# Decoder layer with paged cache: value fetches of a sequence held, on both issuing queues, until the last four key blocks of the next sequence have landed

## The chip, the cores and the metric

One Trainium2 chip; the kernel runs on one of its cores. The metric is the device time of one launch in microseconds (us), lower is better. Where several runs are given, it is their median.

## The reference, cut to what matters

One layer of a hybrid decoder is computed for a prompt of 512 positions and for 8 decoding sequences with one new token each, which have 4096 past positions in a paged cache (128 positions to a page, 256 to a block, so 16 blocks a sequence). The change touches the decoding attention alone:

```python
def moba_sample(q, k, v, cache_k, cache_v, page_table):
    ...
        k_full = cache_k[page_table[:, :own_first]].astype(f32).reshape(Bd, n_full, MOBA_BLOCK, H, D)
        kmean = jnp.mean(k_full, axis=2)
        gate = jnp.einsum('bhtd,bnhd->bhtn', qf, kmean)
        _, sel = lax.top_k(gate, topk)
        ...
        kg = cache_k[pages, :, hidx].reshape(Bd, H, T, topk * MOBA_BLOCK, D)
        vg = cache_v[pages, :, hidx].reshape(Bd, H, T, topk * MOBA_BLOCK, D)
        ...
    p = jax.nn.softmax(jnp.concatenate(scores, axis=-1), axis=-1)
    ...
```

All keys of a sequence are read, since every block's mean key is compared with the query. Of the values only those of the three best blocks of each of the 8 heads are read. Everything else of the layer is there too: one input projection of 1024 by 3584 (seven pieces of 512 columns: k, q, v, u, va, ga, gb), the prompt's own attention, the chunked gate of group A, the output projection, norms, and the rows k, v and sgu_v as outputs.

## The kernel before, in words

**Engines and steps.** `make_plan` lists the steps of every engine in lanes (a lane is a list of steps in a fixed order), gives each step a duration and what it waits for, and merges the lanes of an engine greedily by a model clock. Each engine then issues its list in exactly that order. The model has a pseudo-engine Q for the DMA engines, with lanes for keys, values and weights. The plan only orders; what is waited for at run time are semaphores.

**Prompt.** For each of the seven projection pieces, TensorE does four tiles (`pj`, line 957, 8 matmuls each), and for the output projection eight tiles more (`op`, line 1047, 64 matmuls). ScalarE (`ACT`) evacuates, GpSimd (`POOL`) makes the reciprocal roots (`rstd`, lines 833 and 834), VectorE (`DVE`) scales. Prompt attention (`qk`, `ptr`, `pv`, lines 1003, 1012 and 1024) lies between the projection pieces.

**Decoding, for each sequence b of 8.**
1. `ld`: GpSimd issues 16 indirect DMAs of 512 KB (line 820), one for each key block, into K, which is there once. They may start when step `ex` of the sequence before has read K to the end (`s_ext`). Each block has a semaphore `s_k[n]`.
2. `ks`: VectorE adds the two halves of each block (line 684); `gs`: TensorE sums them over partitions, four blocks at a time (line 1063).
3. `ga`, `pg`: VectorE multiplies by the query, picks the top three and their pages (lines 1445 to 1480); the page numbers stand in selT and raise `s_sel`.
4. `ex`, `sr`: VectorE multiplies the picked key blocks by the query (24 products, line 1492) and reduces (line 1507). When `ex` is done, the next sequence's keys may be loaded and SP spreads the next query row over the partitions (`qb`, line 748).
5. `bc`, `mt`, `mb`: bias, maximum, exponent, going through one PSUM bank DC (lines 1070 to 1079 on TensorE, 1512 to 1532 on VectorE, 1253 on ScalarE).
6. `fetch`: 48 DMAs of 32 KB bring the picked values into V, which is there once too. It is fetched by halves of heads (hh) and rank (k). For sequences 0 to 6, ranks 0 and 1 are issued by SP (32 DMAs) and rank 2 by GpSimd (16 DMAs); for the last sequence SP, GpSimd and ScalarE share them (`v_queue`). A half may be fetched when `pv0` or `pv1` of the sequence before has read it (`wait_v_free`). `fetch_v` reads page numbers from selT into registers (line 665) and issues (line 669).
7. `pv0`, `pv1`: TensorE multiplies the exponents by the values (line 1092), ScalarE copies out (lines 1276 and 1277), and SP gathers the rows (`obs`).

**What orders the value fetches.** Each engine's program is in order: SP's fetches stand between its other DMAs, GpSimd's behind the 16 key loads of the next sequence (the plan's `more` holds them back until `ld` 15 of b + 1 has been issued), and only `s_sel` and `wait_v_free` are waited for at run time.

After `pv1` of the last sequence a tail (`fin0` to `ffd`) finishes the sample rows: normalise, gate, output projection in two halves, norm, residual, store.

Of the kernel before, what the change touches and what calls it, by code (L numbers as in the profile page):

```python
# [17 lines left out]
B = 8  # L18
# [30 lines left out]
def make_plan():  # L49
# [175 lines left out]
    for b in range(B):  # L225
        for n in range(NB):
            deps = [("DVE", ("ex", b - 1, PARTS - 1))] if b else []
            add("POOL", "load", ("ld", b, n), 1.25, *deps)
            add("Q", "key", ("k", b, n), KEY_US, ("POOL", ("ld", b, n)))
            deps = [("Q", ("k", b, n))]  # L230
            if n < SUMS and b:
                deps.append(("DVE", ("sr", b - 1)))
            if n >= SUMS:
                deps.append(("PE", ("gs", b, (n - SUMS) // 4)))
            add("DVE", "gate", ("ks", b, n), 0.75, *deps)
        if b == 0:
            add("POOL", "load", ("const",), 8.5)
        for g in range(G):
            late = [("DVE", ("ks", b, n)) for n in range(4 * g, 4 * g + 4)]
            add("PE", "gate", ("gs", b, g), 1.0, *late, *([("DVE", ("ga", b - 1))] if b else []))  # L240
        used = [("Q", ("v", b - 2, hh, k)) for hh in range(2) for k in range(TOP)] if b >= 2 else []
        add("DVE", "gate", ("ga", b), 3.3, ("PE", ("gs", b, G - 1)), ("SP", ("qb", b)), *used)
        parts = [("ex", b, i) for i in range(PARTS)]
        for s in ([("pg", b)] + parts if b == B - 1 else parts[:1] + [("pg", b)] + parts[1:]) + [("sr", b)]:
            deps = [("ACT", ("mb", b - 1))] if s[0] == "sr" and b else []
            add("DVE", "gate", s, {"ex": 1.7, "pg": 1.2, "sr": 3.4}[s[0]], *deps)
        if b:
            add("SP", "spread", ("qb", b), 3.0, ("DVE", ("ex", b - 1, PARTS - 1)))
        add("PE", "score", ("bc", b), 0.3, ("DVE", ("pg", b)), ("DVE", ("sr", b)))
        add("DVE", "score", ("bc", b), 1.2, ("PE", ("bc", b)), ("POOL", ("const",)))  # L250
        add("PE", "score", ("mt", b), 0.3, ("DVE", ("bc", b)))
        add("DVE", "score", ("mt", b), 0.9, ("PE", ("mt", b)))
        add("PE", "score", ("mb", b), 0.3, ("DVE", ("mt", b)))
        add("DVE", "score", ("mb", b), 0.4, ("PE", ("mb", b)))
        add("ACT", "score", ("mb", b), 0.5, ("DVE", ("mb", b)))
        add("DVE", "score", ("pv0", b), 0.2, ("ACT", ("mb", b)))
        landed = []
        for hh in range(2):
            free = [("PE", (f"pv{hh}", b - 1))] if b else []
            landed.append([])  # L260
            for k in range(TOP):
                eng = v_queue(b, k)
                more = [("POOL", ("ld", b + 1, NB - 1))] if eng == "POOL" and b < B - 1 else []
                add(eng, "fetch", ("fetch", b, hh, k), 7.0, ("DVE", ("pg", b)), *free, *more)
                add("Q", "value", ("v", b, hh, k), 1.8, (eng, ("fetch", b, hh, k)))
                landed[hh].append(("Q", ("v", b, hh, k)))
        for hh in range(2):
            s = (f"pv{hh}", b)
            add("PE", "score", s, 1.4, ("ACT", ("mb", b)), ("DVE", ("pv0", b)), *landed[hh])
            stored = [("SP", ("obs", b - 2))] if b >= 2 and hh == 0 else []  # L270
            add("ACT", "score", s, 0.5 + 0.3 * hh, ("PE", s), *stored)
        add("SP", "gather", ("obs", b), 2.0, ("ACT", ("pv1", b)))
# [93 lines left out]
def hymba_kernel(nc, x_prompt, x_sample, cache_k, cache_v, page_table, g_pre, w_in, sgu_gain, sgu_w,  # L366
# [34 lines left out]
    with ctx:  # L401
# [284 lines left out]
        def wait_v(eng, b, hh):  # L686
# [3 lines left out]
            if by_pool:  # L690
                eng.wait_ge(s_vp[hh], 16 * 4 * 2 * by_pool)

        def wait_v_free(eng, b, hh):
            if b >= 1:
                eng.wait_ge(dc_full, dc_use[(f"pv{hh}", b - 1)] + 1)
# [3 lines left out]
        def _(sp):  # L699
# [18 lines left out]
            for s in PLAN["SP"]:  # L718
# [9 lines left out]
                elif kind == "vrow":  # L728
                    t = s[1]
                    if t < NT:  # L730
                        pa_evac_wait(sp, ("pj", 2, t))
                        sp.dma_start(vp_rows[t], v[:, t, :]).then_inc(s_vrow_stored, 16)
                    else:
                        sb_evac_wait(sp, ("sfd", 2))
                        sp.dma_start(vs_rows, vs[:, :]).then_inc(s_vrow_stored, 16)
                elif kind == "vns":
                    sp.wait_ge(s_vns, 1)
                    sp.dma_start(sv_rows, vns[:, :]).then_inc(s_vns_stored, 16)
                elif kind == "qst":
                    sb_evac_wait(sp, ("sfd", 1))  # L740
                    sp.dma_start(q_rows, qs[:, :]).then_inc(s_qst, 16)
                elif kind == "qb":
                    b = s[1]
                    if b == 0:
                        sp.wait_ge(s_qst, 16)
                    else:
                        sp.wait_ge(s_ext, b)
                    sp.dma_start(qb[:, :], q_rows[b:b + 1, :].broadcast_to([P, W])).then_inc(s_qb, 16)
                elif kind == "fetch":
                    b, hh, k = s[1:]  # L750
                    sp.wait_ge(s_sel, b + 1)
                    wait_v_free(sp, b, hh)
                    fetch_v(sp, b, hh, [k], "vs")
                elif kind == "obs":
                    b = s[1]
                    sp.wait_ge(dc_free, dc_use[("pv1", b)] + 1)
                    for j in range(4):
                        sp.dma_start(obs[b:b + 1, :].rearrange("b (t j d) -> b t j d", t=2, j=4)[:, :, j, :],
                                     osb[32 * j:32 * j + 1, b % 2:b % 2 + 1, :].rearrange("a b (t d) -> a (b t) d", t=2)
                                     ).then_inc(s_obs[b % 2], 16)  # L760
                elif kind == "tail":
                    sp.wait_ge(dc_free, dc_use[("pv1", B - 1)] + 1)
                    sp.dma_start(den[:, :], denr[:, :, :]).then_inc(s_tail, 16)
                    sp.wait_ge(s_scr, B)
                    sp.dma_start(xs2_sb, xs_rows.rearrange("b (a c) -> b a c", a=4)).then_inc(s_tail, 16)
                elif kind == "yrow":
                    t = s[1]
                    sp.wait_ge(s_yo, t + 1)
                    sp.dma_start(y_rows[t], xres[t].rearrange("p a b -> p (a b)")).then_inc(s_store, 16)
# [9 lines left out]
        def _(pool):  # L779
# [77 lines left out]
            for s in PLAN["POOL"]:  # L857
# [10 lines left out]
                elif kind == "fetch":  # L868
                    b, hh, k = s[1:]
                    pool.wait_ge(s_sel, b + 1)  # L870
                    wait_v_free(pool, b, hh)
                    fetch_v(pool, b, hh, [k], "vp")
                elif kind == "pj":
# [733 lines left out]
```

## Time and profile before

| | |
|---|---|
| median of 3 runs | 524.53 us |
| lowest and highest of them | 517.46 and 530.83 us |
| the profiled execution, its own time | 516.84 us |
| its span, first instruction to last | 515.1 us |
| mean granted share of TensorE's clock | 0.923 |
| bytes read from HBM | 106.11 MB, 214 GB/s over the span |
| TensorE, VectorE, GpSimd, ScalarE busy | 436.1, 281.0, 242.3, 124.9 us |

Busy time counts matmuls and arithmetic; waiting, branching and issuing DMAs from SP or ScalarE are not counted as busy, GpSimd's DMA issues are. The chain of work is followed back from the last instruction, at each step to what released it; "another core or an unknown queue" there, on one core, is time before an instruction for which the trace shows no other releaser. "Idle before" in a group's row is the idle time of that engine just ahead of the group's instructions.

### The profile page before, as it was taken

Reading aid. Unit: us, or ns where it says so; the run is one execution under the profiler, and the core shown is the slowest. Engines: PE = TensorE matmul, PEld = TensorE weight load, DVE = VectorE, ACT = ScalarE, POOL = GpSimd, SP = SyncE. Lnnn points to the kernel's source line nnn. Section 1 sums busy time; section 2 is a strip of 40 time slices with the busy share of each in tenths; the row PEclk is TensorE's granted clock in tenths of the full one; section 3 lists DMA queues with packets and bytes.
Section 4 is the critical chain, followed back from the end, with each engine's and each line's share of the span. In section 5 each row is a group of like instructions: output and inputs, shape, how many; then the busy total and the mean of one; then the engine's idle time right before and its main releaser. Section 6 shows DMA issues by size and latency. Waiting matters only on the chain.

```text
span 515.1 us, 7913 instructions
## 1 busy us (share of the span) xinstructions
PE 436.1 (85%) x2264; PEld 192.2 (37%) x2264; DVE 281.0 (55%) x749; ACT 124.9 (24%) x290; POOL 242.3 (47%) x356
## 2 busy tenths in 40 slices
PE   6989983999389985999739997799798997798993
PEld 3423431343034532555324543234333343243430
DVE  1535732366055764969445585559542674658253
ACT  2411100000123524553222544142122111000112
POOL 5875277105840054911763117862578357517111
PEclk9989997999699985999955999899999998899998
DMA  8995499545996069911998009993899169924121
GB/s 286 400 394 180 165 382 380 74 165 164 391 283 204 7 198 296 288 15 43 341 391 187 1 22 342 382 335 87 270 303 360 24 232 373 327 30 106 63 81 43
DMA packets 76698, 110.95 MB, mean 215 GB/s; under 512 B 44568, under 2 KB 45080, under 8 KB 76656
## 3 DMA queue, kind: packets, MB, share of 16 engines
q0 software_dynamic: 22576, 71.45, 39.6%
q1 hardware_dynamic: 42720, 21.14, 16.5%
q10 hardware_dynamic: 11360, 17.86, 10.3%
q8 instruction: 18, 0.29, 0.2%
q14 instruction: 24, 0.20, 0.1%
HBM read 106.11 MB, written 4.29 MB: 214 GB/s over the span
## 4 chain that ended last, share of the span: by engine, by line
PE 36%; DVE 14%; another core or an unknown queue 13%; DMA 12%; issue 9%; POOL 8%; ACT 2%; DVEq 2%; ACTq 1%; SPq 1%; POOLq 0%
PE PA L957 17%; DMA K<-in_cache_k,kidx 10%; POOL K L820 6%; PE PA L1047 5%; PE GB L1063 5%; DVE ksum L1492 3%; PE SB L1003 3%; PE PO L1024 2%; DMA V<-in_page_table 1%; DVE ksum L684 1%; PE SB L1012 1%; POOL rstd L834 1%; PE SB L911 1%; DVEq L1490 1%
## 5 line engine op out<-in xcount | busy, mean ns | idle before, releaser
L820 POOL DMA_INDIRECT K<-in_cache_k,kidx x128 | 128.3, 1002 | 146.3 <-DVE ksum L1492 110.8
L957 PE MATMUL PA<-wbuf,hT 128*128 128x512 f32 x384 | 189.0, 634 | 0.0
L684 DVE TENSOR_TENSOR ksum<-K 128x512 f32<-128x512 f32 x128 | 85.1, 688 | 72.3 <-DMA K<-in_cache_k,kidx 54.2
L957 PEld LDWEIGHTS PA<-wbuf,hT 128*128 128x128 f32 x384 | 72.1, 200 | 94.7 <-issue 93.6
L669 POOL DMA_DIRECT2D V<-in_cache_v x128 | 75.5, 594 | 49.9 <-issue 38.9
L1047 PE MATMUL PA<-wbuf,hT 128*128 128x512 f32 x128 | 61.6, 622 | 0.1
L1063 PE MATMUL GB<-ksum,win 128*32 128x512 f32 x256 | 39.6, 675 | 16.4 <-DVE ksum L684 12.3
L1492 DVE TENSOR_TENSOR ksum<-K,qb 128x128 f32<-128x128 f32 x192 | 42.0, 286 | 11.4 <-issue 5.9
L833 POOL TENSOR_SCALAR rstd<-msum 128x1 f32<-128x1 f32 (+3 forms) x24 | 7.9, 330 | 62.3 <-ACT junk L1136 36.6
L1047 PEld LDWEIGHTS PA<-wbuf,hT 128*128 128x128 f32 x128 | 23.3, 194 | 28.3 <-issue 27.7
L1024 PE MATMUL PO<-v,pT 128*128 128x64 f32 x160 | 23.9, 284 | 7.9 <-DVE yb L1410 7.4
L1398 DVE SCALAR_TENSOR_TENSOR pr<-alibi,SB 128x128 f32<-128x128 f32 (+3 forms) x32 | 15.5, 484 | 26.8 <-PE SB L1003 13.8
L957 PE MATMUL PA<-hT,wbuf 128*128 128x512 f32 x64 | 29.2, 600 | 0.0
L1003 PE MATMUL SB<-kT,qT 64*128 64x128 f32 (+3 forms) x64 | 28.1, 525 | 0.0
L971 PE MATMUL SB<-spart,fold 128*8 128x512 f32 x18 | 11.8, 743 | 19.3 <-ACT spart L1264 9.9
L1024 PEld LDWEIGHTS PO<-v,pT 128*128 128x128 f32 x160 | 22.8, 209 | 12.7 <-issue 12.5
L1507 DVE TENSOR_REDUCE sc<-ksum 128x48 f32<-128x3072 f32 x8 | 26.8, 3352 | 0.2
L1236 ACT ACTIVATE pr<-pr,smax 128x128 f32<-128x128 f32 (+3 forms) x32 | 17.9, 560 | 32.8 <-DVE smax L1401 29.7
L1244 ACT COPY pT<-SB 128x128 f32<-128x128 f32 (+3 forms) x32 | 13.4, 421 | 48.7 <-remote 25.7
L1012 PE MATMUL SB<-ident,pr 128*128 128x128 f32 x80 | 16.4, 305 | 6.7 <-ACT pr L1236 6.7
L1063 PEld LDWEIGHTS GB<-ksum,win 128*32 128x32 f32 x256 | 5.6, 113 | 40.4 <-DVE ksum L684 23.2
L911 PE MATMUL SB<-wbuf,hTs 128*32 128x512 f32 x144 | 18.7, 639 | 2.3 <-DMA wbuf<-in_w_in 2.3
(186 smaller groups left out, 377.7 us busy)
## 6 DMA issues: line engine op xcount, KB each, us to landing
wbuf<-in_w_in ACTq DMA_DIRECT2D x5, 2048.0 KB
V<-in_cache_v SPq DMA_DIRECT2D x240, 32.0 KB
V<-in_cache_v POOLq DMA_DIRECT2D x128, 32.0 KB, 6.3
wbuf<-in_w_out ACTq DMA_DIRECT2D x2, 2048.0 KB
wbuf<-in_w_in SPq DMA_DIRECT2D x4, 512.0 KB, 8.2
wbuf<-in_w_in SPq DMA_DIRECT2D x1, 2048.0 KB
K<-in_cache_k,kidx POOLq DMA_INDIRECT x128, 12.6
qb<-q_rows SPq DMA_DIRECT2D x8, 256.0 KB
```

The lines of the kernel that those rows point to most:

```text
L669: eng.dma_start(V[j * ROWS:(j + 1) * ROWS, h * TOP + k, :, :], v_pages[bass.ds(page, 1), :, :, h * HD:(h + 1) * HD] .rearrange("a p r d -> ...
L684: eng.tensor_tensor(ksum[:, n % SUMS, :], K[:, n, 0, :], K[:, n, 1, :], ALU.add).then_inc(s_dsum, 1)
L820: pool.indirect_dma_start(K[:, n, :, :].rearrange("p r w -> p (r w)"), None, k_rows, bass.IndirectOffsetOnAxis(ap=kidx[:, b, n:n + 1], axis=0)
L911: last = pe.matmul(bank[32 * j:32 * j + 32, :], src[:, kc, :], w[:, kc, :], start=(kc < 4), stop=(kc >= 4), tile_position=(0, 32 * j))
L957: last = pe.matmul(bank[:, :], lhs, rhs, start=(kc == 0), stop=(kc == KC - 1))
L1003: sb_filled(pe.matmul(bank[:, 0:(i + 1) * P], qT[o:o + HD, h // 2, i * P:(i + 1) * P], kT[o:o + HD, h // 2, 0:(i + 1) * P], start=True, st ...
L1012: last = pe.transpose(bank[:, jt * P:(jt + 1) * P], pr[:, a % 2, jt * P:(jt + 1) * P], ident[:, :])
L1024: last = pe.matmul(PO[:, i * HD:(i + 1) * HD], pT[:, a % 2, jt, :], v[:, jt, h * HD:(h + 1) * HD], start=(jt == 0), stop=(jt == i))
L1047: last = pe.matmul(bank[:, :], hT[:, kc, t * P:(t + 1) * P], wbuf[:, c % 2, kc, :], start=(kc == 0), stop=(kc == KC - 1))
L1063: last = pe.matmul(GB[32 * j:32 * j + 32, :], win[:, 31 - g:63 - g], ksum[:, (4 * g + j) % SUMS, :], start=(g == 0), stop=(g == G - 1), ti ...
L1492: last = dve.tensor_tensor(kq[:, h * TOP + k, :, :], K[:, bass.ds(n, 1), :, h * HD:(h + 1) * HD] .rearrange("p a r d -> p (a r) d"), qb[:, ...
L1507: dve.tensor_reduce(sc[:, :, :, :].rearrange("p h k r -> p (h k) r"), kq[:, :, :, :], AX.X, ALU.add).then_inc(s_scr, 1)
```

## The change

The value fetches of sequence b (b up to 6) now wait, on SP and on GpSimd, for the semaphores of key blocks 12 to 15 of sequence b + 1. The plan's dependency of every such fetch is set to the landing of key block 15, which gives other orders on all engines.

```diff
@@ make_plan
                 eng = v_queue(b, k)
-                more = [("POOL", ("ld", b + 1, NB - 1))] if eng == "POOL" and b < B - 1 else []
+                more = [("Q", ("k", b + 1, NB - 1))] if b < B - 1 else []
                 add(eng, "fetch", ("fetch", b, hh, k), 7.0, ("DVE", ("pg", b)), *free, *more)
@@ hymba_kernel
+        def keys_landed(eng, b):
+
+            if b < B - 1:
+                for n in range(NB - 4, NB):
+                    eng.wait_ge(s_k[n], 16 * (b + 2))
+
@@ SP's program
                     sp.wait_ge(s_sel, b + 1)
+                    keys_landed(sp, b)
                     wait_v_free(sp, b, hh)
@@ GpSimd's program
                     pool.wait_ge(s_sel, b + 1)
+                    keys_landed(pool, b)
                     wait_v_free(pool, b, hh)
```

The first place is SP, from the third prompt key row stored to the first value fetch of sequence 0. Of before:

```order
L724 DMA out<-yb 128x512 [waits pa_free1]
L724 DMA out<-yb 128x512 [waits pa_free0]
L665 TENSOR_LOAD selT [waits selection_ready]
L667 ISA
L669 DMA V<-in_cache_v 64x2x64
```

and of the changed kernel, whose lines are six higher below the new function:

```order
L730 DMA out<-yb 128x512 [waits pa_free1]
L754 DMA qb<-q_rows 128x512 [waits selected_k_times_q]
L741 DMA out<-vs 8x512 [waits sb_free1]
L665 TENSOR_LOAD selT [waits k_block_loaded14,k_block_loaded13,k_block_loaded15,k_block_loaded12,selection_ready]
L667 ISA
L669 DMA V<-in_cache_v 64x2x64
```

The spread of the next query row (line 748, now 754) and the store of the sample's value row have moved ahead of the first value fetch, and the fetch waits for four key blocks.

The second place is TensorE from the last sum of key blocks of sequence 7 (GB, line 1063, now 1071) onwards. PA with line 1047 (now 1055) is the output projection, two matmuls to a quarter tile; DC with lines 1070, 1075 and 1079 (now 1078, 1083 and 1087) is `bc`, `mt` and `mb`, with line 1092 (now 1100) it is `pv0` or `pv1`. Of before:

```order
L1063 MATMUL GB<-ksum,win 32x512 x4
L1047 MATMUL PA<-wbuf,hT 128x512 x2
L1092 MATMUL DC<-V,pex 32x64 x24
L1047 MATMUL PA<-wbuf,hT 128x512 x4
L1087 MATMUL DC<-psm,one 1x8
L1092 MATMUL DC<-V,pex 32x64 x24
L1047 MATMUL PA<-wbuf,hT 128x512 x4
L1070 MATMUL DC<-spread,one 128x24
```

and of the changed kernel:

```order
L1071 MATMUL GB<-ksum,win 32x512 x4
L1055 MATMUL PA<-wbuf,hT 128x512 x4
L1095 MATMUL DC<-psm,one 1x8
L1100 MATMUL DC<-V,pex 32x64 x24
L1055 MATMUL PA<-wbuf,hT 128x512 x2
L1078 MATMUL DC<-spread,one 128x24
L1055 MATMUL PA<-wbuf,hT 128x512 x14
L1083 MATMUL DC<-ident,mx 8x128
L1055 MATMUL PA<-wbuf,hT 128x512 x2
L1087 MATMUL DC<-dgm,one 128x8
L1055 MATMUL PA<-wbuf,hT 128x512 x4
L1100 MATMUL DC<-V,pex 32x64 x24
```

Before, both products with the values of sequence 6 and then `bc` of sequence 7 stand behind this sum. Now `pv1` of sequence 5 and `bc`, `mt`, `mb` of sequence 6 stand there first. Behind the sum, 40 projection matmuls were left in the order of before, and 26 are left now, of 64 for the whole output projection.

## Rows read from the trace of the kernel before

**Rows 1.** The page: busy times, DMA busy tenths in 40 slices, chain by engine.

```profile
PE 436.1 (85%) x2264; PEld 192.2 (37%) x2264; DVE 281.0 (55%) x749; ACT 124.9 (24%) x290; POOL 242.3 (47%) x356
...
DMA  8995499545996069911998009993899169924121
...
PE 36%; DVE 14%; another core or an unknown queue 13%; DMA 12%; issue 9%; POOL 8%; ACT 2%; DVEq 2%; ACTq 1%; SPq 1%; POOLq 0%
```

**Rows 2.** Chain that ended last: start us, us, what; five of its longest.

```profile
73.05 11.37 another core or an unknown queue
...
129.63 13.58 another core or an unknown queue
...
189.28 8.66 another core or an unknown queue
...
254.29 10.71 another core or an unknown queue
...
359.41 10.44 another core or an unknown queue
```

**Rows 3.** Windows, one for each key load: us, busy by engine, clock, DMA share, GB/s.

```profile
13.00:45.00 32.00, 28.94 (x127) 11.14 (x126) 16.68 (x29) 8.52 (x14) 25.46 (x43) 0.95 1.00 374
61.00:93.00 32.00, 22.81 (x70) 8.63 (x69) 12.27 (x22) 2.00 (x4) 23.08 (x29) 0.89 1.07 361
120.00:152.00 32.00, 21.28 (x63) 7.41 (x62) 10.84 (x20) 5.45 (x7) 22.58 (x29) 0.84 0.98 317
183.00:217.00 34.00, 26.21 (x116) 12.24 (x105) 20.98 (x46) 14.41 (x33) 22.82 (x28) 0.80 0.89 285
242.00:277.00 35.00, 23.89 (x85) 11.98 (x84) 16.19 (x33) 8.50 (x20) 22.61 (x29) 0.69 1.00 336
307.00:345.00 38.00, 32.18 (x119) 13.43 (x111) 20.37 (x44) 13.34 (x37) 29.57 (x37) 0.96 0.98 340
361.00:401.00 40.00, 35.16 (x143) 13.89 (x141) 16.15 (x28) 8.15 (x17) 28.28 (x35) 0.96 0.96 306
416.00:451.00 35.00, 28.02 (x147) 12.19 (x145) 20.06 (x35) 4.46 (x11) 24.73 (x32) 0.90 1.04 340
```

**Rows 4.** Timeline of SP's queue and of ScalarE, sequence 0's values.

```profile
65.42 25.34 SPq L669 DMA_DIRECT2D V<-in_cache_v  x16
...
92.34 6.03 SPq L669 DMA_DIRECT2D V<-in_cache_v  x8
...
84.44 0.58 ACT L1264 COPY spart<-SB 128x512 f32<-128x512 f32 x1 [11.39 <-remote]
```

**Rows 5.** Groups of lines 1047 and 820, and the landing times of line 820.

```profile
L1047 PE MATMUL PA<-wbuf,hT 128*128 128x512 f32 x128 | 61.6, 622 | 0.1
...
L820 POOL DMA_INDIRECT K<-in_cache_k,kidx x128 | 128.3, 1002 | 146.3 <-DVE ksum L1492 110.8
...
DMA to landing us min/median/max: 6.1/12.6/16.6
```

**Rows 6.** Timeline of the last sequence: last key issue, last key sums, scores, fetch, products.

```profile
436.53 0.93 POOL L820 DMA_INDIRECT K<-in_cache_k,kidx  x1 [0.31 <-issue]
437.46 4.76 POOL L669 DMA_DIRECT2D V<-in_cache_v  x8
...
450.23 2.49 DVE L684 TENSOR_TENSOR ksum<-K 128x512 f32<-128x512 f32 x4
...
469.20 3.35 DVE L1507 TENSOR_REDUCE sc<-ksum 128x48 f32<-128x3072 f32 x1
...
463.66 13.77 SPq L669 DMA_DIRECT2D V<-in_cache_v  x16
...
480.16 0.88 PE L1092 MATMUL DC<-V,pex 128*32 128x64 f32 x48
...
482.90 0.86 PE L1092 MATMUL DC<-V,pex 128*32 128x64 f32 x46
```

**Rows 7.** Timeline of TensorE in the tail.

```profile
499.09 1.98 PE L1047 MATMUL PA<-wbuf,hT 128*128 128x512 f32 x4
```

## Prediction

> **What bounds the kernel now.** I read the page first [rows 1]. TensorE is busy for 436.1 of 515.1 us, and the DMA engines go from full slices to nearly empty ones and back. So nothing is full all the time: TensorE has 79 us of idle time, and the question is where that lies. The chain by engine has a strange entry: 13% of the span (some 66 us) is charged to a releaser that the trace doesn't know, on a kernel of one core.
>
> The chain in order of time shows where these pieces are [rows 2]. The five longest make 54.8 us, each 9 to 14 us long. The windows are the eight stretches in which the keys of a sequence are loaded, from first issue to last landing [rows 3]; four of the pieces lie inside one, and the fifth begins 2 us ahead of one and ends inside. In the first one the DMA engines are full (share 1.00, 374 GB/s) and TensorE is still busy for 28.9 of 32 us, 90%. In the other seven the DMA engines are just as full, but TensorE is busy for 189.6 of 246 us, 77%. At the first window's 90% it would be 222 us. The difference, 32 us, is idle time that a full DMA system alone doesn't explain. What the seven have and the first has not is value fetches issued by SP while GpSimd issues key loads.
>
> SP's queue shows the same thing from the other side [rows 4]. Eight value DMAs take 6.03 us when GpSimd no longer issues keys (0.75 us each); the sixteen issued from 65.42 on take 25.34 us. In the same stretch ScalarE stands still for 11.39 us before 84.44 with a releaser called remote, though the matmuls that it copies from had run some 12 us before. Such a piece ends, in my reading, when GpSimd's burst of 16 key issues ends. I call it the crawl. That it comes from SP's fetches and key issues running together is an inference from eight windows, not shown.
>
> **The change, part by part.** I make the sum against the profiled execution, 516.84 us (its span of 515.1 and 1.7 around it). That execution lies below the lowest of the three runs; I add the sum to their median, 524.53 us.
>
> *Idle time that goes.* The values of b can't be issued any more while keys of b + 1 are. What they now meet is the start of the load of b + 2. On SP a sequence's 32 issues cost 32 x 0.75 = 24 us from the landing of keys of b + 1. The next key load starts once gate and selected scores are done: the last sums of sequence 7 start at 450.23 and its score reduce at 469.20 [rows 6], so some 19 us behind the landing. With the wait for V to be free, the last 8 to 12 of the 32 issues therefore still run beside the first 5 to 10 us of the next load. The new order says the same: the spread of the next query row, which waits for the end of `ex`, stands ahead of the last group of eight. Load 1 has nothing beside it at all. Of the 32 us, I take two thirds, 22, as gained: 32 is the end where no crawl is left, 0 the end where it comes with the key loads whatever SP does.
>
> *Shorter key loads.* The seven windows are 32 to 40 us long, and 8.4 MB at the first window's 374 GB/s takes 22.4. A landing takes a median of 12.6 us from its issue [rows 5]. With values out of the way a load may be 2 to 4 us shorter. TensorE's in-order program hides it, since most of the key sums wait for their turn there; I count 0 (ends: 0 and -10).
>
> *TensorE's work that moves ahead of the last key sum.* The plan thinks that values land late and fills TensorE with projection instead. Behind the last key sum stood 40 output projection matmuls, and now 26. The trace has 128 records and 61.6 us for the 64 [rows 5], 0.96 us each, so 14 x 0.96 = 13.5 us of work now precede this sum. `pv1` of sequence 5 (0.9 us) and `bc`, `mt`, `mb` of 6 (1 us or so) move behind it. Net +11 us, on the path as TensorE is 85% busy there.
>
> *The tail.* This is the surest loss. In the trace the last keys are in K at about 450.5 (issue at 436.53, landing median, first of the four last sums at 450.23), and `pv1` of sequence 7 ends at 483.8 [rows 6]: 33 us, as the values of sequence 6 were fetched before. Now all 48 of them start at 450.5. SP needs 24 to 26 us with the row stores between, they land at +27. TensorE has 25 us of projection to do after the key sums, and VectorE `bc`, `mt`, `mb` of 6 and then `sr` of 7, which bring `pv1` of 6 to +33. Only then may the second half of V be fetched for sequence 7; the sixteen issues of SP in the trace take 13.77 us, so the last value lands near +46 and `pv1` of 7 ends near +47.5, that is 14.5 later. What follows it gets 5 us shorter: three pieces of projection like the one at 499.09 (1.98 us) [rows 7] lie in the tail's chain now and are done by then in the new order. Net +9 us.
>
> *The waits themselves.* SP waits with nothing urgent behind it: row stores, `obs`, and `qb`, which stands ahead where it matters. GpSimd is different. Behind its waiting fetch are the reciprocal roots of va, ga and gb, for which VectorE and then ScalarE and TensorE's PA banks wait, and the next 16 key issues. It idles 110.8 us waiting for `ex` in seven pieces [rows 5], 16 us each. Now it has the 19 us from landing to the end of `ex`, less 16 x 0.6 = 9.5 us of issues (eight take 4.76 us [rows 6]) and a wait of perhaps 5 us for `pv1` of the sequence before. That fits with some 5 us to spare, if TensorE isn't late. I put +5 for all of it (ends: 0 and +12).
>
> Sum: -22 + 0 + 11 + 9 + 5 = +3 us. 524.5 + 3 = 527.5.
>
> A rule speaks for less than that on the gain side. The trace has full DMA engines in the first window without the idle time, which agrees with it, and sixteen issues in 25.34 us, which it doesn't explain. By the rule alone the first term would be 0; that is the third case below.
>
> **The rivals.**
>
> *A. No crawl at all, and shorter loads.* Value issues beside the first few microseconds of a load do no harm: four of the five pieces begin 6 to 12 us after a load's start [rows 2, 3], as if the queues must fill first. Then the terms are -32 and -10, with 11, 9 and 0 to 5: -20 us, 504. For it: load 1 is cleared altogether, and the pieces were on the chain. Against it: TensorE's own 436 us and some 40 us of the new tail in which it has almost nothing to do already make 475, and each wait for keys or ScalarE comes on top.
>
> *B. The stalls stay, or come back elsewhere* (the slower side). They belong to key loads beside anything, or value issues that hang over into the next load are slowed to 1.6 us each (25.34 / 16) and stretch through it. Then the first term is 0 and the moved work, the tail and the waits are paid in full: 11 + 9 + 8 = +28, 552. It decides from the point at which less than 18 us of idle time is won. For it: after the second load the last eight issues always stand behind `qb`, so at the load's start; and windows 6 and 7 (85% and 88% busy) show little idle time to win. Against it: the first window.
>
> *C. GpSimd becomes late.* If `pv1` of the sequence before comes more than 5 us late, the next key issues move by as much, seven times. 5 us each would be +35 in place of the +5; with the 22 won, +33 or 558. Against it: the order puts `pv1` within a tile or two behind the key sums. I count it into B's chance.
>
> **How the numbers follow.** The forecast case (-8 to +10 us, 527.5) has 0.40; A 0.29; B with C 0.31. A measurement of this kernel can tell about 2%, 10.5 us, from no change. Faster by more: 0.27 from A and 0.03 from the forecast's edge, 0.30. Within: 0.34 and 0.02, 0.36. Slower: 0.31 and 0.03, 0.34. Cases of both signs hold most of the chance, so the likeliest one's own range is 516 to 535; the range for 8 in 10 reaches from below A to B's time, 502 to 552.
>
> **What would show it.** In the changed kernel's windows of key loads TensorE should be busy near 85 to 90%, and the entry with no known releaser fall from 13% to under 5% of the chain; sixteen value issues on SP should take 12 to 14 us. If that entry stays at 10% or more, B holds. From the landing of sequence 7's last keys to the end of `pv1` of 7 there should be 45 to 50 us in place of 33, and to the end of the span 73 in place of 64.6. GpSimd's first key issue of each sequence should still be released by VectorE's line 1492 (now 1500); if it directly follows value issues, C holds. The forecast is wrong if the tail costs less than 5 us or the idle time in loads doesn't change.

## The result and the profile after it

| | before | changed |
|---|---|---|
| median of 4 runs, us | 523.06 | 537.15 (534.51 to 541.16) |
| ratio | 1 | 1.031 [1.019, 1.044] |
| profiled execution, us | 516.84 | 538.43 |
| its span, us | 515.1 | 536.6 |
| mean granted clock | 0.923 | 0.897 |

The change makes the kernel about 3% slower: +14 us between the medians, +21.6 between the profiled executions. (The profiled execution before lies 6 us below its median, the changed one 1 us above, so a part of the 21.6 is spread between executions.) 537 lies inside the range, and on the slower side of the 527.5 that was forecast.

First the page of the changed kernel (span, busy times, DMA tenths, chain by engine), to be held against [rows 1].

```profile
span 536.6 us, 7995 instructions
...
PE 434.7 (81%) x2264; PEld 196.9 (37%) x2264; DVE 281.3 (52%) x749; ACT 122.6 (23%) x288; POOL 242.7 (45%) x356
...
DMA  8994596539963980039922499639947982133400
...
PE 47%; issue 15%; DMA 8%; DVE 8%; POOL 6%; another core or an unknown queue 6%; SPq 4%; ACT 3%; ACTq 2%; DVEq 1%; POOLq 0%
```

TensorE does the same work in the same time (434.7 against 436.1 us) and is idle for 101.9 us instead of 79.0. Two windows of the tail, from the last key sum on TensorE to the end, show where that idle time is. The first row is of the kernel before:

```profile
457.00:515.10 58.10, 47.62 (x334) 19.43 (x326) 29.98 (x82) 9.33 (x30) 14.32 (x28) 0.97 0.23 65
```

The second is of the changed kernel:

```profile
461.00:536.60 75.60, 40.65 (x361) 18.67 (x353) 30.40 (x89) 9.04 (x29) 19.33 (x36) 0.74 0.22 61
```

Idle time in the tail went from 58.10 - 47.62 = 10.5 us to 75.60 - 40.65 = 35.0, by 24.5 us. That is all of the difference, and slightly more. The rest of TensorE's idle time, outside the tail and the seven later key loads, is 12.1 us before and 12.2 now. The tail became 17.5 us longer with 7.0 us less to do in it (its granted clock falls from 0.97 to 0.74). The key loads, from which the gain was to come, hardly changed. These are the seven windows (first issue to last landing) that answer to the last seven of [rows 3]:

```profile
62.00:91.00 29.00, 21.89 (x67) 8.12 (x66) 12.17 (x22) 1.72 (x4) 14.97 (x16) 0.88 0.92 358
119.00:150.00 31.00, 29.62 (x89) 11.07 (x87) 15.93 (x24) 6.66 (x13) 17.29 (x16) 1.00 0.97 346
172.00:200.00 28.00, 15.61 (x53) 8.83 (x52) 6.97 (x13) 5.26 (x12) 14.73 (x16) 0.71 0.94 324
...
sum 220.00, PE 165.28 PEld 73.81 DVE 97.73 ACT 43.22 POOL 118.00; mean PE 23.61 PEld 10.54 DVE 13.96 ACT 6.17 POOL 16.86
```

TensorE is busy in them for 165.28 of 220 us, 75% (77% before). Their idle time is 54.7 us in place of 246 - 189.6 = 56.4. Window 2 is clean, and windows 3 and 4 (15.49 of 28 us) are worse than any of before.

The stalls of [rows 2] are there too. Part of them now carries another name, as these four of the longest pieces of the chain show (start, us, what):

```profile
177.17 10.91 issue
...
250.50 12.12 issue
...
314.55 12.37 another core or an unknown queue
...
429.12 8.46 another core or an unknown queue
```

The unknown releaser fell from 13% to 6%, but "issue" (time in which the engine waited for nothing that the profile shows) rose from 9% to 15%. An entry of the chain can shrink because the same stall is booked under another, and the two together stayed at 21 to 22%. They are read together below.

The sharpest row is in load 1, the load of sequence 1's keys. The changed SP has no value fetch in it at all, as its queue shows (a query row, a row store, and values from 91.03 only):

```profile
61.27 0.33 SPq L754 DMA_DIRECT2D qb<-q_rows  x1
86.34 0.30 SPq L741 DMA_DIRECT2D out<-vs  x1
91.03 2.20 SPq L669 DMA_DIRECT2D V<-in_cache_v  x3
```

Yet ScalarE and VectorE stand as before, at the same place and for as long as in [rows 4] (11.39 us before 84.44 there). Their timelines, with the idle time ahead of a row in brackets:

```profile
83.08 0.59 ACT L1272 COPY spart<-SB 128x512 f32<-128x512 f32 x1 [11.44 <-remote]
84.62 0.69 DVE L1351 SCALAR_TENSOR_TENSOR qT<-PA,pT 128x512 f32<-128x512 f32 x1 [10.12 <-remote]
```

**The tail.** SP's queue in the last two sequences:

```profile
446.07 26.81 SPq L669 DMA_DIRECT2D V<-in_cache_v  x24
480.02 6.12 SPq L669 DMA_DIRECT2D V<-in_cache_v  x8
490.57 6.22 SPq L669 DMA_DIRECT2D V<-in_cache_v  x8
498.24 6.16 SPq L669 DMA_DIRECT2D V<-in_cache_v  x8
```

TensorE in the same stretch:

```profile
443.77 1.50 PE L1100 MATMUL DC<-V,pex 128*32 128x64 f32 x48
460.49 1.06 PE L1071 MATMUL GB<-ksum,win 128*32 128x512 f32 x8
465.14 0.86 PE L1100 MATMUL DC<-V,pex 128*32 128x64 f32 x46
468.17 12.28 PE L1055 MATMUL PA<-wbuf,hT 128*128 128x512 f32 x28
488.06 0.86 PE L1100 MATMUL DC<-V,pex 128*32 128x64 f32 x46
495.87 0.62 PE L1078 MATMUL DC<-spread,one 8*128 8x24 f32 x2 [6.95 <-ACT osb L1285]
506.04 1.49 PE L1100 MATMUL DC<-V,pex 128*32 128x64 f32 x46
```

The keys of sequence 7 have landed at 441.5, 9 us earlier than before, and nothing is made of it. The values of sequence 6 start at 446.07, two microseconds behind the first product of sequence 5 (443.77), which frees their buffer. Their second half can only start behind the second product, at 465.14 and thus behind the last key sum. Products of 6 end near 489, those of 7 at 507.5: 47.0 us from the last key sum to there (460.49 to 507.5), against 27.3 before (456.54 to 483.8). What follows is 29.1 us instead of 31.3. It holds far less TensorE work than before, but what is left runs at a lower clock: the last stretch has a granted share of 0.62 (0.94 before), and its first group of sixteen sample projection matmuls, with TensorE idle for 9.93 us shortly before, takes nearly twice as long. Of before, and of the changed kernel:

```profile
497.23 1.92 PE L911 MATMUL SB<-wbuf,hTs 128*32 128x512 f32 x16
```

```profile
519.61 3.64 PE L919 MATMUL SB<-wbuf,hTs 128*32 128x512 f32 x16 [0.36 <-issue]
```

VectorE shows the link of which the prediction had only half:

```profile
474.75 1.30 DVE L1500 TENSOR_TENSOR ksum<-K,qb 128x128 f32<-128x128 f32 x6
...
483.22 3.35 DVE L1515 TENSOR_REDUCE sc<-ksum 128x48 f32<-128x3072 f32 x1 [0.38 <-ACT pex L1261]
```

The products for the scores of sequence 7 are ready at 474.75 + 1.30 = 476.05 but reduced at 483.22 only, since `sr` stands in order behind the softmax of 6 (469.20 before, right behind `ex` [rows 6]).

**GpSimd** was not late. These are the groups of its key issues and value issues, to be held against [rows 5]:

```profile
L827 POOL DMA_INDIRECT K<-in_cache_k,kidx x128 | 127.5, 996 | 78.8 <-DVE ksum L1500 43.1
...
L669 POOL DMA_DIRECT2D V<-in_cache_v x128 | 76.3, 596 | 103.6 <-issue 94.7
```

It now waits 94.7 us ahead of value fetches and 43.1 (110.8 before) for VectorE's `ex`. The key issues of a sequence start no more than 1 us later than before.

### The profile page after: what moved, and what is told of

Read it like the earlier page. It is cut to its first block, busy times and chain, and to the rows that moved or that the text cites. A ratio compares the mean times of both kernels' runs of the same rounds, so it can differ in the third digit from the quotient of the medians.

```text
span 536.6 us, 7995 instructions
## 1 busy us (share of the span) xinstructions
PE 434.7 (81%) x2264; PEld 196.9 (37%) x2264; DVE 281.3 (52%) x749; ACT 122.6 (23%) x288; POOL 242.7 (45%) x356
## 4 chain that ended last, share of the span: by engine, by line
PE 47%; issue 15%; DMA 8%; DVE 8%; POOL 6%; another core or an unknown queue 6%; SPq 4%; ACT 3%; ACTq 2%; DVEq 1%; POOLq 0%
PE PA L965 23%; PE PA L1055 7%; DMA K<-in_cache_k,kidx 6%; POOL K L827 4%; PE GB L1071 4%; PE SB L1011 3%; SPq L669 3%; PE SB L919 2%; PE PO L1032 2%; PE SB L1020 2%; DVE ksum L1500 2%; PE DC L1100 1%; DMA V<-in_page_table 1%; PE SB L979 1%
## 5 line engine op out<-in xcount | busy, mean ns | idle before, releaser
L827 POOL DMA_INDIRECT K<-in_cache_k,kidx x128 | 127.5, 996 | 78.8 <-DVE ksum L1500 43.1
L669 POOL DMA_DIRECT2D V<-in_cache_v x128 | 76.3, 596 | 103.6 <-issue 94.7
L684 DVE TENSOR_TENSOR ksum<-K 128x512 f32<-128x512 f32 x128 | 83.6, 687 | 60.7 <-DMA K<-in_cache_k,kidx 27.9
L1071 PE MATMUL GB<-ksum,win 128*32 128x512 f32 x256 | 38.1, 633 | 9.0 <-DVE ksum L684 7.6
L1032 PE MATMUL PO<-v,pT 128*128 128x64 f32 x160 | 23.6, 282 | 10.3 <-issue 9.7
L979 PE MATMUL SB<-spart,fold 128*8 128x512 f32 x18 | 11.5, 727 | 17.6 <-ACT spart L1272 10.5
L919 PE MATMUL SB<-wbuf,hTs 128*32 128x512 f32 x144 | 22.4, 724 | 2.9 <-DMA wbuf<-in_w_in 2.5
L1020 PEld LDWEIGHTS SB<-ident,pr 128*128 128x128 f32 x80 | 9.7, 149 | 33.8 <-issue 24.2
```

Of the source, the lines that this page charges most:

```text
L669: eng.dma_start(V[j * ROWS:(j + 1) * ROWS, h * TOP + k, :, :], v_pages[bass.ds(page, 1), :, :, h * HD:(h + 1) * HD] .rearrange("a p r d -> ...
L684: eng.tensor_tensor(ksum[:, n % SUMS, :], K[:, n, 0, :], K[:, n, 1, :], ALU.add).then_inc(s_dsum, 1)
L827: pool.indirect_dma_start(K[:, n, :, :].rearrange("p r w -> p (r w)"), None, k_rows, bass.IndirectOffsetOnAxis(ap=kidx[:, b, n:n + 1], axis=0)
L919: last = pe.matmul(bank[32 * j:32 * j + 32, :], src[:, kc, :], w[:, kc, :], start=(kc < 4), stop=(kc >= 4), tile_position=(0, 32 * j))
L1020: last = pe.transpose(bank[:, jt * P:(jt + 1) * P], pr[:, a % 2, jt * P:(jt + 1) * P], ident[:, :])
L1032: last = pe.matmul(PO[:, i * HD:(i + 1) * HD], pT[:, a % 2, jt, :], v[:, jt, h * HD:(h + 1) * HD], start=(jt == 0), stop=(jt == i))
```

## The experiments

Ratios are to the kernel before, measured beside each kernel on the same chip. In four of the kernels the profiled execution was apart from the median: by 13 us in `values_own_lane`, 7 in `keys_in_flight5`, 6 in `keys_in_flight8` and 4 in `own_lane_in_flight6`. Of `own_lane_in_flight6` and `keys_in_flight5` no row is used.

**Which part of the change costs, its order or its waits?** The first kernel keeps the changed order and drops the waits at run time:

```diff
-                    keys_landed(sp, b)
-                    keys_landed(pool, b)
```

> The changed kernel's order on every engine, without the waits for the four key blocks at run time. If the loss is the order's (TensorE's projection ahead of the last key sums and the scores put off to the tail), this stays slow: 530 to 540 us, with 70 us or more from the last key sum to the end of the span. If it is the run-time waits' (values fetched late, GpSimd blocked), it comes back to 518 to 526 us. In this order SP can fetch early, so the entry with no known releaser should come back to some 13% of the chain if SP's fetches make it, and stay near 6% if the order does.

Measured: 533.15 us, 1.023 [1.012, 1.034]. The order alone makes most of the loss. The rest, up to 1.031, lies within the intervals. From the last key sum to the end it takes some 76 us, as with the waits (58.6 before). The unknown releaser has 11% of the chain and "issue" 10%, 21% together as in the two other kernels, so the entry that was to tell the fetches from the order doesn't tell them apart.

The second has the waits of the change in the order of before:

```diff
-                more = [("Q", ("k", b + 1, NB - 1))] if b < B - 1 else []
+                more = [("POOL", ("ld", b + 1, NB - 1))] if eng == "POOL" and b < B - 1 else []
```

> The order of the kernel before, with the waits at run time. If the order is the loss, this is within 2% of before: 518 to 530 us. If late values are the loss it is at least as slow as the changed kernel, 535 to 560 us, since TensorE then stands at products whose values have not come, while in the changed order it has projection to do. I expect the second: before, pv0 began only 2 to 17 us after the values had landed, and the wait moves their landing by 10 to 25 us.

Measured: 574.97 us, 1.102 [1.093, 1.111]. TensorE's timeline around one of the products shows where it stands:

```profile
508.86 0.88 PE L1100 MATMUL DC<-V,pex 128*32 128x64 f32 x48
509.66 3.70 PE L1055 MATMUL PA<-wbuf,hT 128*128 128x512 f32 x8
522.24 0.17 PE L1095 MATMUL DC<-psm,one 128*1 128x8 f32 x1 [8.88 <-issue]
```

In the old order the second product stands shortly behind the key sums, its values are just being fetched, and TensorE stands for 8.9 us in front of it. So the order is not a side effect that could be left away: a wait of this kind needs an order made for it, and the order has its own price in the tail.

**Is the last wait, that of sequence 6, the price of the tail?** The change for sequences 0 to 5 only, in plan and in waits:

```diff
-            if b < B - 1:
+            if b < B - 2:
```

> The change for sequences 0 to 5 alone; the fetches of sequence 6 go as before, in the plan and at run time. If the tail carries the loss, as the trace says (from the last keys landed to the end 95 us against 64.6), this returns 12 to 22 us of it: 516 to 526 us. If the loss is spread over the sequences, 530 to 537 us.

Measured: 534.56 us, 1.022 [1.010, 1.034]; 2.6 us came back, and not the 12 to 22 that were expected. The keys of sequence 7 landed at 438.7, and the values of 6 were fetched at 442.7 anyway, since the first product of 5, which frees their buffer, came only at 440. By then the whole decoding chain is one sequence late. Giving the last sequence its freedom back doesn't undo that.

**What makes the stalls?** Since they stay where SP fetches nothing, what is left in common is the key transfers of 512 KB each, which GpSimd issues 1.24 us apart without a limit. A landing takes 12.6 us in the median [rows 5], so some ten of the sixteen are under way late in a load; that is an estimate, 12.6 / 1.24. (The landing times come from the last two or three blocks of each load; of the others the trace lacks events.) The next kernel is the one before, in its own order, with at most six allowed. Where the limit acts it also spaces the issues, so the number under way and their pace change together:

```diff
             def load_k(m):
                 b, n = divmod(m, NB)
+                if n >= 6:
+                    pool.wait_ge(s_k[n - 6], 16 * (b + 1))
```

> The kernel before, in which GpSimd issues key block n of 6 to 15 only when block n - 6 of the same sequence has landed, so that at most 6 key transfers (3 MB) are under way. Theory 1 (the stalls of 9 to 14 us come from a deep backlog of key transfers, with or without SP's fetches): the stalls shrink, TensorE's idle time in the seven key loads falls from 56 us towards 25, and the kernel gets faster, 495 to 515 us. Theory 2 (they come from SP's value fetches beside any key issues): they stay, and the time is 520 to 530 us. Theory 3 (keys are short of bandwidth already, so that a limit starves the queues): slower, 530 to 550 us.

Measured: 489.38 us, 0.939 [0.929, 0.948], faster than the range of any of the three theories. The chain of this kernel by engine, the first key window behind sequence 0's, and the sum over the seven:

```profile
PE 49%; DMA 13%; DVE 13%; issue 8%; POOL 7%; another core or an unknown queue 4%; DVEq 2%; ACTq 1%; ACT 1%; SPq 1%; POOLq 0%
```

```profile
60.00:93.00 33.00, 33.00 (x110) 12.75 (x109) 17.09 (x29) 1.84 (x4) 23.32 (x28) 1.00 1.08 356
...
sum 253.00, PE 220.00 PEld 93.58 DVE 137.10 ACT 64.56 POOL 177.25; mean PE 31.43 PEld 13.37 DVE 19.59 ACT 9.22 POOL 25.32
```

With the same value fetches beside the keys and the DMA engines as full (1.08), TensorE is busy for all 33 us of the window in which it had lost 9. Over the seven it is 87%. This load takes 33 us in place of 32, and the seven together 253 in place of 246. The landing line of the key loads shows what changed:

```profile
DMA to landing us min/median/max: 6.2/8.6/10.8
```

A median of 8.6 us instead of 12.6 [rows 5], again of the last blocks of a load: with 356 GB/s against 361 the transfers don't move faster, they queue for less time.

Not every stall is gone. Two long pieces are left in the chain, and at the first of them TensorE, ScalarE and VectorE stood together, for 8.39, 9.18 and 9.09 us:

```profile
169.65 9.07 another core or an unknown queue
330.71 10.78 another core or an unknown queue
```

```profile
170.08 0.94 POOL L822 DMA_INDIRECT K<-in_cache_k,kidx  x1 [0.30 <-issue]
```

```profile
179.52 0.66 PE L1026 MATMUL PO<-v,pT 128*128 128x64 f32 x2 [8.39 <-DVE yb L1412]
```

It begins about the sixth key issue of its load (170.08), before the limit has held back any of them (173.96), so six under way are enough for a stall. It ends 2.3 us behind the tenth issue, after which GpSimd paused. The second piece is another thing: ScalarE alone waits there, for a product, and TensorE is idle for 2.0 us of it. The piece at 359.41 in [rows 2] is of that kind too, with TensorE idle for 2.6 of its 10.44 us, so the five pieces of the prediction are four stalls.

Three more depths, with the same edit and 8, 4 and 5 for the 6:

> The kernel before with 8 key transfers allowed in place of 6. If depth of the backlog makes the stalls, this lies between: 495 to 515 us, with TensorE's idle time in the key loads between that of 6 and that of no limit. If only the spacing of GpSimd's issues mattered, it would equal 6 (489 us) or before (520 us).

> The kernel before with 4 key transfers allowed (2 MB). Stalls at their least; but 2 MB over a landing time of 6 us or so is 350 GB/s, so key loads should get longer by 10% or more. If stalls are all that counts: 480 to 488 us. If the load's length counts as much: 490 to 505 us.

> The kernel before with 5 key transfers allowed. 4 gave 497.9 us, 6 gave 489.4, 8 gave 514.0. If stalls go down to a floor at 6 and only the load's length counts below it, 490 to 495 us; if it is all stalls with a minimum between, 483 to 489 us.

| in flight at most | ratio | median, us | TensorE busy in the seven windows |
|---|---|---|---|
| no limit (before) | 1 | 518.9 to 522.1 | 77% |
| 8 | 0.991 [0.987, 0.995] | 514.04 | 79% |
| 6 | 0.939 [0.929, 0.948] | 489.38 | 87% |
| 5 | 0.932 [0.923, 0.940] | 488.68 | |
| 4 | 0.953 [0.943, 0.962] | 497.87 | 88% |

Eight removes little, but it also hardly acts: GpSimd waits for landings 7 times and 5.8 us in all, against 21 times and 21.0 us with six. So the gap between eight and six is where the limit begins to act, and no more can be read from it. Four removes as much idle time as six, and there the loads themselves become the wait: GpSimd stands 75.0 us for landings. Five and six can't be told apart. Either beats both kernels of this case.

**Do value fetches make stalls at all?** Kernel before, but only sequence 0's values are fetched. The decoding output of sequences 1 to 7 is computed from sequence 0's values, so 336 of the 384 value DMAs and their traffic are left out:

```diff
         def fetch_v(eng, b, hh, ks, which):
+            if b >= 1:
+                return
...
         def wait_v(eng, b, hh):
+            b = 0
```

> The kernel before, whose value fetches of sequences 1 to 7 are left out (336 of 384 DMAs; the products go on with sequence 0's values), so that key loads 2 to 7 have no value fetch beside them. If value fetches on SP made the stalls (the prediction's crawl), TensorE's idle pieces of over 3.5 us in loads 2 to 7 go, and the time falls to 485 to 495 us. If the backlog of keys makes them by itself, pieces of 7 to 14 us stay in loads 2 to 7, and the time falls only by what the values took: 505 to 518 us.

Measured: 500.86 us, 0.959 [0.951, 0.967]. The stalls are still on the chain:

```profile
74.64 10.00 another core or an unknown queue
132.64 8.41 another core or an unknown queue
248.50 7.38 another core or an unknown queue
344.32 10.50 another core or an unknown queue
417.58 5.21 another core or an unknown queue
```

The first of them lies in load 1, beside which sequence 0's values are still fetched. Those at 132.64 and 248.50, in loads 2 and 4, have no value fetch near them, and VectorE and ScalarE both stood there (5.79 and 7.40 us in load 4). At 344.32 ScalarE alone waits, as at 359.41 in [rows 2]. The unknown releaser and "issue" have 9% each (13% and 9% before), and TensorE is busy for 82% of the seven windows. 500.86 us lies between the ranges of the two cases. So value fetches aren't needed for a stall, and the slow issues on SP are a sign of it and not its source. Whether the fetches add to the stalls isn't shown: part of the 21 us may be the traffic and the issues saved.

**The change with the limit.** The changed kernel with at most six in flight:

> The changed kernel with the same limit of 6 key transfers under way. If the stalls have one cause (the backlog of keys) and the change's loss another (its order), the two add up: 0.939 x 1.031 = 0.968 of before, some 504 us, and TensorE's idle pieces of 7 to 12 us in the key loads go. If the change's loss was made by stalls (a full backlog beside TensorE's new order), it vanishes with them: 488 to 494 us. If the order sets the end whatever the stalls, no gain: 520 us or more.

Measured: 516.53 us, 0.994 [0.988, 0.999]. TensorE is busy for 86% of the windows, but from the last key sum to the end it is still 76 us. The unknown releaser and "issue" have 2% and 15% of the chain, 17% together (21% without the limit). The limit gives the change 21 us where it gave the kernel before 31, so the two effects don't simply add up (that would have been 504 us). It leaves the change 5.5 points behind the same limit without it (0.994 against 0.939).

**Why the order is bad.** In the plan's model keys, values and weights share one serial lane "Q". With the change the values stand in it behind the next keys, land late by the model, and the planner moves products and scores a sequence back on every engine. This gives the values a lane of their own in the model, waits kept:

```diff
-                       ("Q", "key value weight")):
+                       ("Q", "key weight"), ("QV", "value")):
...
-                add("Q", "value", ("v", b, hh, k), 1.8, (eng, ("fetch", b, hh, k)))
+                add("QV", "value", ("v", b, hh, k), 1.8, (eng, ("fetch", b, hh, k)))
```

> The changed kernel, waits and all, but its plan no longer thinks that values queue behind the next sequence's keys (values have a model queue of their own). Run-time waits are the same; the order changes: TensorE's products pv0 and pv1 come earlier against the key sums, and 48 output projection matmuls are behind the last key sum's group, not 26. If the plan's belief that values land late makes the loss, this returns most of it: 518 to 528 us. If late values themselves do, TensorE now stands waiting for them as in the kernel with the waits alone: 545 to 575 us.

Measured: 517.69 us beside 518.91 before, with the four runs in two groups, 504.50 and 512.05, 523.33 and 525.62. Too wide for a ratio, but no slower than before. What the expectation says of 48 projection matmuls behind the last key sum was wrong, there are 46; that changes nothing in it. A plan that knows better removes the loss of the change. Its profiled execution, the fastest of the four, has 84% in the windows with no limit on the keys, more than before. What stands beside a load, and when, may matter as well; but its landing median is 8.6 us, as low as with six in flight, so fewer keys were under way there too.

The same without the waits:

> The order of values_own_lane without the waits for the four key blocks at run time. values_own_lane, with them, took 517.7 us, level with before. If the waits do no harm in an order that allows for them, this is within 1% of that, 513 to 523 us. If they hold TensorE up by a few us a sequence, it is 500 to 512 us. If they do good (values out of the key loads), it is slower than 523 us.

Measured: 513.74 us in 12 runs, 0.988 [0.983, 0.992]. Nothing shows that the waits bring anything: without them the median is 4 us less, within the spread of the four runs above.

And with the waits and at most six in flight:

> The changed kernel with values in a lane of their own in the plan, and at most 6 key transfers under way. values_own_lane was level with before (517.7 against 518.9 us). If the waits of the change are free once order and backlog are put right, this equals keys_in_flight6: 485 to 493 us. If the held-back values cost a few us by themselves, 495 to 508 us.

Measured: 508.79 us, 0.970 [0.960, 0.979], a little above the upper of the two ranges. With the limit the best form of the change still costs 3 points against the limit alone (0.939). Whether its waits or its order cost them wasn't taken apart.

## Why the prediction was right, and which step failed

The time lay in the range, and the place of the surest loss was right. But the forecast case didn't come true: what happened is rival B. The terms one by one, by the profiled executions (+21.5 us of span):

- **Idle time in key loads, -22: the step that failed.** Measured -1.7 us (56.4 to 54.7). By the prediction's own sign (the idle time in loads doesn't change) the forecast was wrong. The prediction called it an inference that "it comes from SP's fetches and key issues running together". It rested on one window without fetches, the first, which also has no earlier load, no decoding work and other work on TensorE beside it. Load 1 of the changed kernel has no fetch either, and the stall of 11.4 us is in place. What does move the idle time is a limit on the key transfers under way, 0.939 with every value fetch in its old place in the order. Another reading of the prediction held, that a stall ends when GpSimd's burst of key issues ends: the first four pieces of [rows 2] end 84.42 - 81.01 = 3.4, 3.7, 2.3 and 3.5 us behind the last of an unbroken row of key issues (in load 3 that row stops after ten, at 195.68).
- **Shorter key loads, 0.** First issue to last landing fell from about 35 to 31 us, as estimated (2 to 4), and the last landing came 9 us earlier. TensorE's order hid it: right.
- **Moved work, +11.** The tail has 7.0 us less of TensorE busy time, so the term came to 7. The matmuls moved as forecast, but those left in the tail run slower at the lower clock (3.64 us in place of 1.92, above), for which the prediction had no term. With 1.7 us less idle time and 1.4 us less busy time overall this gives the 4 us by which the last key sum came later (456.54 to 460.49). No term for GpSimd is left in this sum.
- **The tail, +9: mis-sized, +17.5 measured.** The sum had `pv1` of 7 14.5 us later, from the landing, and counted SP's 48 issues from there. It missed that the second half of V for 6 waits for `pv1` of 5 at 465, 23.6 us behind the landing; that `sr` of 7 waits for `pex` of 6; and that `bc` of 7 waits 6.95 us for a copy by ScalarE, which issues value fetches too. What follows `pv1` of 7 got 2.2 us shorter instead of 5. Counted from the last landing, as in the prediction's test, `pv1` of 7 ended 66.0 us behind it (45 to 50 forecast) and the span 95.1 us behind it (73 forecast).
- **The waits on GpSimd, +5.** 0 by the sum above. The first key issue of a sequence is still released by VectorE's line 1500, so C is out.

That 537 lies in the range is in part luck: the range is 50 us wide, and it holds the times of the forecast, of A and of B alike. The misses by term are +20.3 for the idle time, -4 for the moved work, +8.5 for the tail, -5 for GpSimd and -1.4 of busy time, which takes the forecast of +3 to 21.4, measured 21.5.

The tests that were named in advance point to B, and one was badly chosen. TensorE was busy for 75%, not 85 to 90%. The unknown entry came to 6%, between the marks of 5 and 10%, because stalls were rebooked as issue. The last sixteen issues of SP for sequence 0 still lie beside the load of sequence 2's keys, as these rows of its queue in the changed kernel show, and take 19.5 us and not 12 to 14:

```profile
120.06 6.33 SPq L669 DMA_DIRECT2D V<-in_cache_v  x8
126.41 0.38 SPq L738 DMA_DIRECT2D out<-v  x1
129.52 13.20 SPq L669 DMA_DIRECT2D V<-in_cache_v  x8
```

TensorE was busy for 29.62 of 31 us beside them, so slow issues on SP and an idle TensorE don't always come together. B gave 552 and assumed 8 us for GpSimd; without it and with the measured terms, 7 + 17.5 - 3, it is the 21.5.

As to the rule weighed there (the Trainium skill, DMA: Bandwidth & Descriptors, section Queues, rings and completion order), that each DMA engine takes its queues in turn, packet by packet: the first term that the prediction drew from it, 0, was nearer to the measured -1.7 than the forecast's -22. No run here tests the taking of turns itself.

**What stays open.** Between the transfers and an engine that stands for 10 us with its operands ready lies some part of the chip that no run here shows. The DMA packets in which instructions are fetched are in the trace. Between 62 and 103 us the changed kernel has one of them, done at 75.2, while ScalarE stood until 83.08, so a late one doesn't end that stall. The passing on of semaphores is left, and so is the writing of the trace's own records: every run here has a recorded span and clock, so none shows the chip without them, and of the 2048 landing events of the key blocks the trace of the kernel before holds only 1091. Number under way and unbroken issuing weren't taken apart: a limit of six does both, fewer transfers and pauses in GpSimd's row of issues, and the stalls end shortly behind such a row. A fixed pause between the issues, without a limit, would tell. Neither were bytes and descriptors (smaller key blocks would tell). Depth alone doesn't rank the kernels either: the changed one has a landing median of 9.6 us, thus fewer keys under way than before (12.6), and the same idle time.

## What to carry to other kernels

When several engines stand at once with a releaser that the trace doesn't know, beside full DMA engines, limit how many transfers are in flight before moving any work around them; two lines of code and three depths show whether it helps. A dependency given to a planner is a new order on every engine: run order and waits apart, and look at where the last unit of work ends up. A resource in the planner's model that is stricter than the chip's makes a harmless dependency costly.

## What the runs showed of the hardware that I had not expected

- Beside indirect loads of 512 KB, issued 1.24 us apart (423 GB/s asked, 361 GB/s moved in load 1 [rows 3]), TensorE, ScalarE and VectorE stand four times in the kernel before (9.19, 11.39 and 9.92 us in load 1), while the trace shows nothing that they wait for. Each time it is over 2.3 to 3.7 us behind the last of an unbroken row of issues. With at most eight, six, five and four of them allowed under way the kernel takes 0.991, 0.939, 0.932 and 0.953 of the time.
- A limit of six costs next to nothing in throughput: DMA share 1.08 and 356 GB/s in load 1, against 1.07 and 361 [rows 3].
- Value fetches are issued by SP in 0.75 us each alone and in up to 1.6 us beside key issues (16 in 25.34 us [rows 4]). It isn't the issuing of DMAs that is slow there. Between 75.4 and 83.4 us in the kernel before, three of SP's register instructions of line 667, which touch no DMA, take 0.70 us each, where the same instruction takes 0.053 us on GpSimd:

```profile
L667 POOLq FUSED_REGOPS  x8: 50/53/53, 74.1 to 85.1; - x8
L667 SPq FUSED_REGOPS  x5: 53/697/700, 75.4 to 85.3; - x5
```
